# Sixteen heads of sparse attention taken two at a time in the halves of TensorE's array

## The reference, cut to what matters

```
q, k = rmsnorm per head; g = sigmoid(x @ w_gate)             # 16 heads x 3 branches
for n in (0, 1):                                             # two branches over the full 256 keys
    s = q[h] @ k[n][G].T / 8 - slope[h] * distance           # masked to the past
    o[h] += g[h, 1 + n] * softmax(s) @ v[n][G]
k_c, v_c = gelu(blocks_of_32(k0 + pos) @ w1) @ w2            # 15 compressed keys, values
o[h] += g[h, 0] * softmax(q[h] @ k_c[G].T / 8 - bias) @ v_c[G]
h = h + concat(o) @ w_out
```

## Time and profile before

| what | value |
|---|---|
| median of three runs | 1765.5 us |
| the profiled execution, its own time | 1759.98 us |
| its span in the trace | 1758.0 us |
| TensorE busy | 1729.1 us, 98% |
| VectorE busy | 1108.2 us, 63% |
| ScalarE busy | 908.5 us, 52% |
| GpSimd busy | 158.5 us, 9% |
| read from HBM | 281.26 MB, 161 GB/s |
| mean granted clock of TensorE | 0.996 of full |

### The profile page before, as it was taken

The page is one execution under the profiler, slowest core; times in us unless marked ns, Lnnn a source line. Parts: engine busy times, 40 slices in busy tenths (PEclk is TensorE's granted clock), DMA queues, the critical chain, the costliest instruction groups (busy, mean ns, idle before and its releaser), DMA issues.

```text
span 1758.0 us, 32148 instructions
## 1 busy us (share of the span) xinstructions
PE 1729.1 (98%) x14004; PEld 1661.4 (95%) x14004; DVE 1108.2 (63%) x1487; ACT 908.5 (52%) x1220; POOL 158.5 (9%) x62
## 2 busy tenths in 40 slices
PE   7999999999999999999999999999999999999999
PEld 7999978899999999999988789999999998799999
DVE  6888757565565557765467846555655557756653
ACT  6865577444454445444465545444544446554442
POOL 0000000000022101220000001220122000002210
PEclk9999999999999999999999999999999999999999
DMA  7554332444355455545533205545554564335544
GB/s 271 177 176 146 126 120 97 168 169 167 124 196 187 151 187 206 199 164 180 198 102 133 84 22 195 192 155 185 213 192 170 170 224 136 101 116 195 189 155 134
DMA packets 44635, 284.37 MB, mean 162 GB/s; under 512 B 4944, under 2 KB 6608, under 8 KB 17744
## 3 DMA queue, kind: packets, MB, share of 16 engines
q1 hardware_dynamic: 44352, 282.25, 46.9%
q10 hardware_dynamic: 144, 0.08, 0.0%
HBM read 281.26 MB, written 1.05 MB: 161 GB/s over the span
## 4 chain that ended last, share of the span: by engine, by line
PE 86%; DVE 6%; ACT 5%; issue 2%; DMA 0%; DVEq 0%; ACTq 0%
PE bank L490 85%; ACT WH L1058 2%; DVE WL L1599 2%; ACT SB L1172 0%; DVE HT L1655 0%; ACT SB L1281 0%; DVE STAT L1722 0%; ACT XM L1065 0%; DVE XM L1607 0%; ACT XR L1065 0%; ACT FB L1082 0%; DVE FB L1625 0%; DVE SB L1717 0%; DMA PAR<-in_par 0%; DVE XR L1607 0%
## 5 line engine op out<-in xcount | busy, mean ns | idle before, releaser
L1599 DVE TENSOR_TENSOR WL<-RAW,WH 128x2048 fp32r<-128x2048 f32 (+1 forms) x282 | 590.6, 2096 | 312.0 <-ACT WH L1058 312.0
L490 PE MATMUL bank<-XR,WH 128*128 128x256 f32 x3648 | 651.8, 283 | 11.3 <-DVE WL L1749 10.8
L1058 ACT ACTIVATE WH<-RAW 128x2048 fp32r<-128x2048 f32 (+1 forms) x282 | 493.3, 1752 | 227.7 <-PE bank L490 224.0
L490 PEld LDWEIGHTS bank<-XR,WH 128*128 128x128 f32 x3648 | 561.0, 190 | 17.4 <-DVE WL L1749 10.8
L490 PE MATMUL bank<-XR,WL 128*128 128x256 f32 x1824 | 512.2, 281 | 0.0
L490 PEld LDWEIGHTS bank<-XR,WL 128*128 128x128 f32 x1824 | 346.1, 190 | 0.0
L490 PE MATMUL bank<-XF,WH 128*128 128x256 f32 x1760 | 311.4, 281 | 0.0
L490 PE MATMUL bank<-XM,WH 128*128 128x256 f32 x1664 | 294.7, 281 | 2.7 <-DVE XM L1640 1.6
L490 PEld LDWEIGHTS bank<-XF,WH 128*128 128x128 f32 x1760 | 269.4, 188 | 0.0
L490 PEld LDWEIGHTS bank<-XM,WH 128*128 128x128 f32 x1664 | 254.1, 188 | 4.1 <-DVE XM L1640 2.0
L490 PE MATMUL bank<-XF,WL 128*128 128x256 f32 x880 | 246.9, 281 | 0.0
(11 more groups left out here) (267 smaller groups left out, 1757.4 us busy)
## 6 DMA issues: line engine op xcount, KB each, us to landing
RAW<-in_f1i SPq DMA_DIRECT2D x44, 1024.0 KB, 4.9
RAW<-in_f2i SPq DMA_DIRECT2D x44, 1024.0 KB, 4.9
RAW<-in_w_in SPq DMA_DIRECT2D x35, 1024.0 KB, 4.9
RAW<-in_w_ffn_in SPq DMA_DIRECT2D x22, 1024.0 KB, 4.9
RAW<-in_f1o SPq DMA_DIRECT2D x32, 704.0 KB, 4.1
RAW<-in_f2o SPq DMA_DIRECT2D x32, 704.0 KB, 4.1
RAW<-in_diff_w_in SPq DMA_DIRECT2D x12, 1024.0 KB, 4.9
RAW<-in_w_ffn_out SPq DMA_DIRECT2D x16, 704.0 KB, 4.1
```

The source lines that it names most:

```text
L490: return e.matmul(o, l, r, start=start, stop=stop)
L1058: e.activation(split_at(u, cols)[0], RAW[:, u % NRAW, 0:cols], ACT.Copy).then_inc(hi_done.tick(u), 1)
L1599: e.tensor_tensor(lo, RAW[:, u % NRAW, 0:cols], hi.bitcast(f32), sub).then_inc(lo_done.tick(u), 1)
```

## The change

The loop goes over 16 pairs of maps, p in range(19), in all three lists. TensorE's step p has `score_pair(p)`, then `weigh_pair(p - 3)`, then `turn_pair(p - 2)`, then the fillers. The two heads of a pair lie in the two halves of the array (rows for the scores, columns for the weighing), and their matmuls are issued in turns. The diagonals are gone: `scale_pair` on ScalarE multiplies the 128 x 256 part of the probabilities in place, `settle_pair` on VectorE the 128 x 128 part, and `turn_pair` transposes plainly. Maxima, reciprocals and gates are taken for two maps in one instruction. `compressed_scores` issues its two halves in turns as well. The fillers are put on new steps; the units `nsa_w_in` 2 and 3 come at other places of the stream; the split of unit 4 (`asked(("nsa_w_in", 9))`) is moved from before the loop into step 0, and `nsa_values(1)` likewise to behind the first scores.

```diff
-    add("nsa_w_in", (6, 0, 8, 7, 9, 1, 4, 5))
+    add("nsa_w_in", (6, 0, 8, 7, 9, 1, 4, 5, 2))
     for half in range(2):
         units.append((("cmp_w1", half), A["cmp_w1"][0, half], 2048, True))
-    add("nsa_w_in", (2,))
-    for half in range(2):
-        units.append((("cmp_w1", 2 + half), A["cmp_w1"][1, half], 2048, True))
+    units.append((("cmp_w1", 2), A["cmp_w1"][1, 0], 2048, True))
     add("nsa_w_in", (3,))
+    units.append((("cmp_w1", 3), A["cmp_w1"][1, 1], 2048, True))
...
+            def score_pair(name, p, qh, kh, ready):            # tensor
+                bs = [take("aux", (name, "s", 2 * p + n)) for n in range(2)]
...
+                for n, b in enumerate(bs):
+                    mm(b[:, 0:128], qh(2 * p + n, 0), kh(2 * p + n)[:, 0:128])
+                for n, b in enumerate(bs):
+                    mm(b[:, 128:384], qh(2 * p + n, 1), kh(2 * p + n)).then_inc(scored.tick((name, 2 * p + n)), 1)
...
+            def weigh_pair(name, p, o, v, start=True, stop=True):
...
+                for n in range(2):
+                    mm(o(2 * p + n), v(2 * p + n, 0), ps[n][:, 0:256], start, False)
+                for n in range(2):
+                    mm(o(2 * p + n)[:, 128:256], v(2 * p + n, 1), ps[n][:, 256:384], False, stop).then_inc(weighed.tick((name, 2 * p + n)), 1)
...
+            def turn_pair(name, p):
+                for i in (2 * p, 2 * p + 1):
+                    b = take("aux", (name, "t", i))
+                    q.wait_ge(first_norm, (name, i))
+                    q.wait_ge(p_norm, (name, i, 1))
+                    for c in range(3):
+                        t = e.transpose(b[:, c * 128:c * 128 + 128], slot(name, i)[:, c * 128:c * 128 + 128], ident)
...
+            for p in range(19):                                # tensor
+                if p < 16:
...
+                    score_pair("nsa", p, nsa_q, nsa_k, [(normed, ("q", G)), (kdup_v, (n, 3)), (copied, ("kdup", n, 3))])
+                if 0 <= p - 3:
...
+                    weigh_pair("nsa", p - 3, nsa_o, nsa_v, n == 0 and h % 4 < 2, False)
+                if 0 <= p - 2 < 16:
+                    turn_pair("nsa", p - 2)
+                if p == 0:
+                    nsa_values(1, "third")
+                if p == 1:
+                    nsa_unit(1, ("q", 1))
+                if p == 2:
+                    nsa_unit(4, ("cmp", 0), "second")
+                    nsa_sum(("q", 1))
+                if p == 3:
+                    nsa_unit(5, ("cmp", 1))
+                if p == 4:
+                    nsa_unit(2, ("q", 2))
+                if p in (5, 6):
+                    compress(0, p - 5)
+                if p == 5:
+                    nsa_sum(("q", 2))
+                if p in (7, 9):
+                    compress(1, p // 9, "one")
+                if p == 8:
+                    nsa_unit(3, ("q", 3), "third")
+                    compressed_keys()
+                if p == 9:
+                    compressed_key_sum()
+                    nsa_sum(("q", 3))
+                if p in (11, 12, 13, 14):
+                    compressed_scores(p - 11)
+                if p == 12:
+                    compressed_values()
+                if p in (13, 14, 15, 16):
+                    compressed_turn(p - 13)
+                if p in (14, 15, 16):
+                    compressed_out(p - 14)
+                if p == 16:
+                    nsa_out(0, 0, 2, "first")
+                if p == 17:
+                    nsa_out(0, 2, 4)
+                    nsa_out(1, 0, 4, "second")
+            compressed_out(3)
+            nsa_out(2, 0, 6, "third")
+            nsa_out(0, 4, 6)
+            nsa_out(1, 4, 6)
+            for n in range(3):
+                nsa_out(n, 6, 8)
...
+            def scale_pair(name, p):                           # scalar
+                q.wait_ge(recip, (name, p))
+                for n in range(2):
+                    s = slot(name, 2 * p + n)[:, 128:384]
+                    e.activation(s, s, ACT.Copy, scale=st[:, n, 3:4]).then_inc(p_norm.tick((name, 2 * p + n, 1)), 1)
...
+            for p in range(19):                                # scalar
+                for i in {0: (9,), 1: (1,), 2: (4,), 3: (5,), 4: (2,), 5: (10,), 7: (12,), 8: (3,), 9: (13,), 11: (14,)}.get(p, ()):
+                    asked(("nsa_w_in", i) if i < 10 else ("cmp_w1", i - 10) if i < 14 else ("nsa_w_out", 0))
...
+                    turn_over("nsa", 2 * p - 4)
+                    turn_over("nsa", 2 * p - 3)
+                if p < 16:
+                    score_pair("nsa", p)
+                if 0 <= p - 1 < 16:
+                    scale_pair("nsa", p - 1)
...
+            def settle_pair(name, p, factor=None):             # vector
+                q.wait_ge(expd, (name, 2 * p + 1, 1))
+                e.reciprocal(r, r).then_inc(recip.tick((name, p)), 1)
...
+                for n in range(2):
+                    s = s2[:, n, 0:128]
+                    e.tensor_scalar(s, s, r[:, n, 0:1], None, mult).then_inc(first_norm.tick((name, 2 * p + n)), 1)
...
+            for p in range(19):                                # vector
+                if p < 16:
+                    score_pair("nsa", p)
+                if p in (2, 3, 4, 5, 9):
+                    nsa_scale({2: ("q", 1), 3: ("cmp", 0), 4: ("cmp", 1), 5: ("q", 2), 9: ("q", 3)}[p])
...
+                    settle_pair("nsa", p - 1, gv[:, :, h:h + 2, 1 + n].rearrange("p j h -> p h j"))
...
+                if p in (3, 6, 10):
+                    nsa_q({3: 1, 6: 2, 10: 3}[p])
+                if p in (7, 10):
+                    hidden(p // 10)
+                if p in (8, 11):
+                    gelu(p // 11)
```

More of the change, by code:

```diff
@@ L472, in tensor @@
             q = Queue(e, counting)
-            kinds = {"main": (0, 1, 2), "open": (3,), "aux": (4, 5, 6, 7), "pair": (0, 1), "held": (2, 3), "one": (0,), "three": (1, 2, 3), "second": (2,),
+            kinds = {"main": (0, 1, 2), "open": (3,), "aux": (4, 5, 6, 7), "pair": (0, 1), "held": (2, 3), "one": (0,), "three": (1, 2, 3, 0), "first": (1,), "second": (2,),
                      "third": (3,), "four": (0, 1, 2, 3)}
@@ L865, in compressed_values @@
             def compressed_values():
-                b = take("third", "vc")
+                b = take("aux", "vc")
                 q.wait_ge(cmp_act, ("hr", 1))
@@ L876, in compressed_scores @@
                 q.wait_ge(cmp_v, "kc")
-                for odd in range(2):
[L878 to L884, removed]
+                bs = [take("aux" if odd else "one", ("sc", G, odd)) for odd in range(2)]
+                for j in range(2):
+                    for n in range(2):
+                        at = j * 30 + n * 15
+                        for odd in range(2):
+                            t = mm(bs[odd][:, at:at + 15], head(QN, 4 * G + 2 * n + odd)[:, j * 128:j * 128 + 128],
+                                   KC[odd * 64:odd * 64 + 64, G * 32:G * 32 + 15])
+                            if j == 1 and n == 1:
+                                t.then_inc(cmp_pe.tick(("sc", G, odd)), 1)
+                for odd in range(2):
                     empties(("sc", G, odd), (cmp_v, ("sc", G, odd)))
@@ L919, in tensor, with nsa_q, nsa_k, nsa_o @@
             nsa_sum(("k", 1))
[L920 to L932, removed]
+            def nsa_q(i, j):
+                return head(QN, nsa_map(i)[2])[:, j * 128:j * 128 + 128]
+            def nsa_k(i):
+                _, n, h = nsa_map(i)
+                return kd[n][h % 2 * 64:h % 2 * 64 + 64, h // 4, :]
+            def nsa_o(i):
+                G, _, h = nsa_map(i)
+                return in_bank(("nsa", "o", G))[h % 2 * 64:h % 2 * 64 + 64, h % 4 // 2 * 256:h % 4 // 2 * 256 + 256]
+            def nsa_v(i, s):
+                G, n, _ = nsa_map(i)
+                return vn[n][:, s, G * 64:G * 64 + 64]
+            for p in range(19):
+                if p < 16:
+                    G, n, _ = nsa_map(2 * p)
+                    score_pair("nsa", p, nsa_q, nsa_k, [(normed, ("q", G)), (kdup_v, (n, 3)), (copied, ("kdup", n, 3))])
+                if 0 <= p - 3:
+                    G, n, h = nsa_map(2 * p - 6)
+                    if p % 4 == 3:
                         take("three", ("nsa", "o", G))
@@ L1173, in scores, with score_pair @@
                         expd.tick((name, i, n)), 1)
+            def score_pair(name, p):
+                st = pair_stat(name, p)
+                q.wait_ge(maxed, (name, "pair", p))
+                for n in range(2):
+                    s = slot(name, 2 * p + n)
+                    for j, (a, z) in enumerate(((0, 128), (128, 384))):
+                        e.activation(s[:, a:z], s[:, a:z], ACT.Exp, scale=slope(name, 2 * p + n), bias=st[:, n, j:j + 1],
+                                     accum_out=st[:, n, 2 + j:3 + j]).then_inc(expd.tick((name, 2 * p + n, j)), 1)
+            def scale_pair(name, p):
+                st = pair_stat(name, p)
+                q.wait_ge(recip, (name, p))
```

(14 more changed lines are left out.)

175 lines of the change are left out of this document (77 added, 98 removed).

## The result

The changed kernel took 1736.8 us in the median of four runs (1735.74 to 1744.06), the kernel before beside it 1764.2 (1759.96 to 1776.5): a ratio of 0.9845, interval 0.9806 to 0.9884. The forecast was 1742. The profiled executions took 1735.74 and 1759.98 us, 24.2 apart where 24 were forecast.

The account below looks back on a forecast made before the run. TensorE's list, busy 98% of the span, was taken as the bound: 41 us leave it, 17 return as waits, a gain of 24; from 1765.5 that gives 1741.5, rounded to 1742, range 1733 to 1752.

Parts of the forecast that it names:

- What leaves the list: TensorE in the loop: pairing scores and weighing, plain transposition and compressed scores in turns take 39.9 us off its list.
- The compressed scores: TensorE: 16 instructions in turns take 1.0 us in place of 1.46, 1.8 us less in all.
- Six plain transpositions: TensorE, each pair: printed 0.88 us, 0.81 start to start, against 2 x 0.87 by diagonals; 14.9 us less.
- What the other lists get: Stretch: VectorE gets 18 us less, 100 of its 118; ScalarE 13 more, 105 of its 92.
- Step 4: Unit 2 waits for unit 5's bank, which VectorE empties only behind score_pair(4): 1.3 us of TensorE wait.
- Step 8: compressed_keys waits for gelu, behind the transfer and split of nsa_w_out 0: 2.2 us of TensorE wait.
- Steps 10 to 16: End of loop, small fillers: VectorE bounds steps 10 to 15, TensorE waits 8 there; 12 us with later waits.
- The clock rival: Steps 10 to 16 all run at 1.2 GHz: 15 us back, gain 9, 1756 us; 12%.
- Behind the loop: nsa_out of units 0 and 1 ends later before the last unit, delaying the next stage: 1.5 us.
- the overlap in turns: Rival: halves issued in turns do not overlap in scores and weighing; 19 us come back, gain 12, 1753 us; 8%.
- Not all of the list counts: Answers the rival that all of TensorE's saving counts, only 2 to 5 us given back: 1727 us; 10%.
- Slower by ScalarE's list: Rival: turn_pair waits for scale_pair, queued on ScalarE behind asked and exponentials; with nothing hidden, 1828 us; 7%.

Follow-up runs that it names:

- e1: Changed kernel with scores, weighing and plain transposes of a step's two maps issued singly on TensorE, other lists kept: 1772.0 us, ratio 1.0031.
- e9: Changed kernel with maps handled singly on TensorE and transposed by diagonals in place of plainly: 1765.1 us, ratio 1.0005.
- e3: Changed kernel, still in pairs, but transposed by diagonals again, without the in-place scaling: 1741.4 us, ratio 0.9865.
- e7: Changed kernel with unit 2 on another bank and the splits of nsa_w_out 0, 1 and 2 moved later: 1734.5 us, ratio 0.9824.
- e4: Kernel before with only in-place scaling and plain transposition added, no pairs: 1778.7 us, ratio 1.0078.
- e6: Kernel before with in-place scaling, no pairs, transposing by ordinary matmuls with the identity: 1761.7 us, ratio 0.9994.
- e2: Changed kernel with one head's score and weighing matmuls of a pair issued ahead of the other's, not in turns: 1740.1 us, ratio 0.9864.
- e11: The changed kernel run again, unaltered: 1738.2 us, ratio 0.9853 to the kernel before.
- e5: Changed kernel with every transposition in its pairs an ordinary fp32 matmul by the identity: 1744.3 us, ratio 0.9873.
- e8: Like e7, but pairs from p = 6 on transposed by ordinary matmuls with the identity: 1734.2 us, ratio 0.9818.

## Why the prediction was right

**What leaves the list.** Scores 0.86 and weighing 0.80 for a pair came as read from the back-to-back pairs, and e1 and e9 put the overlap at 25 and 26 us. The compressed scores took 1.00 as estimated (995.59 to 996.59). Six plain transpositions are at 968.47, in front of scores, and at 994.55, in front of compressed scores:

```profile
968.47 0.88 PE L651 MATMUL bank<-CON,FB 128*128 128x128 f32 x6
969.27 0.93 PE L502 MATMUL bank<-FA 64*128 64x128 f32 x8
...
994.55 1.11 PE L651 MATMUL bank<-CON,SB 128*128 128x128 f32 x6
995.59 1.07 PE L502 MATMUL bank<-FB,FA 64*128 64x15 f32 x16
996.59 0.44 PE L938 MATMUL bank<-CON,FB 128*128 128x128 f32 x2
```

The printed 0.88 of six transpositions is the one forecast. What they hold TensorE for depends on what follows: 0.64 in front of a unit, 0.71 in front of `compress`, 0.80 in front of scores (0.81 was the price of the forecast), up to 1.07 among the compressed parts; 0.75 in the mean of the twelve groups at full clock with no wait behind them, so about 1 us more left the list. By diagonals they took 1.36 and 1.54 (e3) in the first and third of these places: the plain form is 1.9 to 2.1 times cheaper. The Trainium skill, "TensorE: Matmul & The Clock Gate", section Terms, says 4 times for fp32; no run here shows more than 2.1. In all 42 us left, where 39.9 were forecast.

**What the other lists get.** VectorE 100.3 busy (forecast 100), ScalarE 101.5 (forecast 105).

**The waits.** Step 4: 1.58 (forecast 1.3), ended by the emptying of the bank, as said. Step 8: 2.87 (forecast 2.2). It shows on ScalarE (timeline), then on VectorE, whose last two rows bear on the next point:

```profile
951.79 1.92 ACT L1118 ACTIVATE WH<-RAW 128x2048 fp32r<-128x2048 f32 x1 [3.13 <-DMA RAW<-in_nsa_w_out]
```

```profile
953.74 2.29 DVE L1678 TENSOR_TENSOR WL<-RAW,WH 128x2048 fp32r<-128x2048 f32 x1 [0.90 <-ACT WH L1118]
956.20 0.90 DVE L2207 RECIPROCAL FB<-FB 128x120 f32<-128x120 f32 x1
957.14 0.35 DVE L2213 TENSOR_TENSOR FB<-FB 128x60 f32<-128x60 f32 x2
...
967.84 1.02 DVE L1818 SCALAR_TENSOR_TENSOR SB<-bank,CON 128x384 f32<-128x384 f32 x2 [1.49 <-PE bank L502]
...
988.68 1.02 DVE L1818 SCALAR_TENSOR_TENSOR SB<-bank,CON 128x384 f32<-128x384 f32 x2 [2.67 <-PE bank L502]
```

The compress of step 7 ended at 946.59; ScalarE has `nsa_w_out` 0 5.2 us later, near the 4.8 of the forecast, then come the two parts of its split, then `gelu`, and TensorE starts at 957.59 behind it. e7 took both waits away and won 6.7 us of stretch, which shows their place.

**Steps 10 to 16** are where the size was right and its make-up wrong. Forecast were 12 us of waits with VectorE as the bound. Found are 5.6 of idle (10.1 less 1.58 and 2.87) and some 7 of low clock (15.6 us of work between 974.6 and 991.7, 46% of it), 12.8 in all. Steps 10 to 15 took 34.9 us (from the scores at 966.81 to the weighing at 1001.73), the 34 of the forecast; TensorE idled 3.6 of them where 10 were forecast. VectorE was busy 29.0, not 32, and itself waited for TensorE, 1.49 (ending in step 10) and 2.67 in the rows above: its list was not the bound for the whole time. The step that failed is the one sentence "It is the bound, and TensorE waits 8": the clock took the place of most of that wait, and e9 against e3 says the same, with 4 of 26 us of added work hidden, not 12. The clock rival, given 12%, came true for 17.1 of the some 39 us, and for 3.4 more in step 8. It did not add to the forecast. The likely reason is that a slower TensorE meets fewer waits, but no run has the plain transposition, full clock and the same lists, so this is not shown, and that the two errors cancelled to within 1 us is luck.

**Behind the loop** a wait of 0.92 stands at 1035.47, in the next stage; 1.5 were forecast. The profiled sums: 24.3 in the stretch, 24.1 in the span, 24 forecast. So the total was right, with a list 2 us better and give-backs 2 us worse, 18.8 in the stretch instead of 17 in all: two more errors that cancel.

The other rivals: the overlap in turns is in the rows, 0.86 and 0.80 for a pair. Not all of the list counts (e3 against after: 11.5 us of list, 0.7 of stretch). Slower by ScalarE's list did not happen: TensorE's idle in steps 0 to 9 is 4.5 us, none of it from `scale_pair`. That half of the change alone does make the kernel slower (e4), by a mechanism that the forecast had only for the whole.

**The clock, as far as it is settled.** In the profiled executions, the two kernels whose TensorE hardly waited in the stretch (before and e6, 1.2 and 1.4 us of idle in all, no wait over 0.59) had no low clock there; every other had some, behind waits of 0.8 to 2.9 in front of small groups. The length of the wait alone does not decide it. Waits of 1.58 in front of a unit of 48 matmuls of 256 columns (921.96), of 2.5 in step 8 of e2 and e11, of 1.84 and 1.16 in e5 and of 1.84 in after (ending at 1004.44) left it at 1.00, while 1.44 in e1 went with 51.2 us at half. How long it stayed low went by what followed: singly and plain 75.1 and 51.2 us (e4, e1); singly with ordinary matmuls 20.5 (e9); pairs and plain 20.5 to 27.3 (after, e2, e11) and 13.7 (e7); pairs with ordinary matmuls 3.4, 3.4 and 10.2 (e3, e8, e5). Each of these is one execution, but the mean clock of all executions keeps the order: singly and plain 0.972 to 0.985, pairs and plain (after, e2, e11) 0.985 to 0.991 but for one of 0.994, pairs with ordinary matmuls (e3, e5) 0.991 to 0.996. So both halves of the change act on the clock, against each other. What in a group decides is open: no run varied the size of the groups, or the waits, alone.

## What to carry to other kernels

Two half-array fp32 matmuls of 128 or 256 columns in opposite halves cost one, in turns or head by head, so pair heads first; the pairing was the whole gain here. Those of 15 columns did not come down to half (16 of them 1.46 before, 1.00 in turns). A cheaper instruction on the bounding engine must be followed to what it uncovers: here 11.5 us of cheaper transposition went into waits and a halved clock. In a stretch of small matmuls look at the granted clock behind each wait, and try to remove or fill the wait behind which it falls. And look at the clock of all executions before reading a cause from one trace.

## What the runs showed of the hardware

- A TensorE that is busy without a gap can stay at half clock for 75 us (e4, its slowest execution) and 51 us (e1).
- Useless matmuls in front of a wait can hold the clock up: six times three of 128 x 128 took 4 us of TensorE, with them 3.4 us of the stretch were at half clock and without them 13.7, and the stretch was 3.0 us shorter (135.0 against 138.0; one execution each, and the medians, 1729.1 and 1734.5, are of different groups of runs).
- At half clock not everything doubles: scores 0.86 to 1.58, a factor of 1.84.
